# The low parts of all weights on GpSimd: a two-block hybrid layer stack on one core

## The reference, cut to what matters

```python
def first_block(x, ...):                      # block 1
    for l in range(2):
        h = _rmsnorm(x, norm_g[l])
        (u_a, v_a, z_a, c_q, c_kv, k_r, z_b, q_c, k_c, v_c, g_c, z_c, gate_logits) = _split_cols(h @ w_in[l])
        y_a = _spatial_gating(u_a, v_a, z_a, ...)
        y_b = _mla(c_q, c_kv, k_r, z_b, ...)          # 8 heads, attention causal by chunks
        y_c = _gla(q_c, k_c, v_c, g_c, z_c, ...)      # gated linear attention, 4 heads
        gates = jax.nn.sigmoid(gate_logits + b_gate[l]).reshape(bn, s, N_BRANCH, d)
        merged = (gates[:, :, 0] * (y_a @ w_branch[l, 0]) + gates[:, :, 1] * (y_b @ w_branch[l, 1])
                  + gates[:, :, 2] * (y_c @ w_branch[l, 2]))
        x = x + merged @ w_out[l]
def hybrid_layer(x, mem, ...):                # block 2, twice
    proj = rms_norm(x, norm_g) @ w_in         # a_q a_k a_v a_g b_q b_k b_v b_g m_q m_g
    # oa: attention over blocks of keys, ob: dilated attention, om: attention over 256 memory rows (mem @ w_mem_kv)
    y = concat([oa * silu(a_g), ob * silu(b_g), om * silu(m_g)])
    return x + y @ w_out
```

## Time and profile before

| | us |
|---|---|
| runs (3) | 1699.03, 1702.03, 1704.10; median 1702.03 |
| profiled execution | 1697.58, span of its instructions 1695.8 |
| TensorE busy | 1619.6 (96%) |
| VectorE busy | 1010.1 (60%) |
| ScalarE busy | 729.2 (43%) |
| GpSimd busy | 57.8 (3%) |
| granted TensorE clock | 0.995 of full |

### The profile page before, as it was taken

One profiled execution on the slowest core, in us unless ns is written; L12 is line 12 of the kernel. 1 busy time (PEld: TensorE's weight loads), 2 busy tenths in 40 slices (PEclk: granted clock), 3 DMA queues, 4 the chain that ended last, 5 costly groups with the idle time before them and its releaser, 6 DMA issues.

```text
span 1695.8 us, 21496 instructions
## 1 busy us (share of the span) xinstructions
PE 1619.6 (96%) x8009; PEld 1321.2 (78%) x8009; DVE 1010.1 (60%) x2246; ACT 729.2 (43%) x1503; POOL 57.8 (3%) x80
## 2 busy tenths in 40 slices
PE   6999999999999999999999999999989999997999
PEld 6878777787777878777787877898767779985667
DVE  4597656444444397757443344576886564778663
ACT  4444443333234443543332424434456553344662
POOL 0000002000001000002000001000000010000000
PEclk9999999999999999999999999999999999999999
DMA  7332121332323332112233323332112233211121
GB/s 219 96 87 75 39 61 53 97 98 90 98 89 89 92 92 87 51 50 63 75 96 91 100 87 112 94 84 68 61 33 68 81 87 99 81 49 45 38 75 62
DMA packets 80883, 136.23 MB, mean 80 GB/s; under 512 B 8190, under 2 KB 33420, under 8 KB 80780
## 3 DMA queue, kind: packets, MB, share of 16 engines
q1 hardware_dynamic: 77264, 129.48, 25.5%
q10 hardware_dynamic: 3516, 5.37, 1.1%
HBM read 132.74 MB, written 2.10 MB: 80 GB/s over the span
## 4 chain that ended last, share of the span: by engine, by line
PE 45%; DVE 13%; ACT 4%; issue 2%; POOL 0%; ACTq 0%; DVEq 0%
PE gemm_bank L695 34%; PE aux_bank L762 3%; PE aux_bank L791 3%; DVE w_lo L1340 2%; PE aux_bank L779 2%; DVE rope L1439 1%; ACT w_hi L1021 1%; DVE head_sums L1392 1%; DVE probs L1495 1%; ACT probs L1068 1%; DVE kT L1479 1%; PE aux_bank L750 1%; DVE probs L1507 1%; DVE product L1758 0%; ACT L1293 0%
## 5 line engine op out<-in xcount | busy, mean ns | idle before, releaser
L1021 ACT ACTIVATE w_hi<-raw 128x512 fp32r<-128x512 f32 (+3 forms) x524 | 305.5, 587 | 681.5 <-PE gemm_bank L695 680.1
L1340 DVE TENSOR_TENSOR w_lo<-raw,w_hi 128x512 fp32r<-128x512 f32 (+3 forms) x524 | 330.7, 636 | 445.0 <-ACT w_hi L1021 443.3
L695 PE MATMUL gemm_bank<-act_hi,w_hi 128*128 128x512 f32 x768 | 318.4, 415 | 14.9 <-DVE product L1758 3.8
L695 PE MATMUL gemm_bank<-act_hi,w_lo 128*128 128x512 f32 x768 | 300.8, 392 | 0.0
L695 PE MATMUL gemm_bank<-act_lo,w_hi 128*128 128x512 f32 x768 | 300.2, 391 | 0.0
L695 PE MATMUL gemm_bank<-w_hi,act_hi 128*128 128x384 f32 (+3 forms) x736 | 269.1, 366 | 6.5 <-DVE bq L1380 2.9
L695 PE MATMUL gemm_bank<-w_hi,act_lo 128*128 128x384 f32 (+3 forms) x736 | 257.4, 350 | 0.0
L695 PE MATMUL gemm_bank<-w_lo,act_hi 128*128 128x384 f32 (+3 forms) x736 | 257.4, 350 | 0.0
L695 PEld LDWEIGHTS gemm_bank<-act_hi,w_hi 128*128 128x128 f32 x768 | 144.6, 188 | 57.1 <-issue 12.7
L695 PEld LDWEIGHTS gemm_bank<-act_lo,w_hi 128*128 128x128 f32 x768 | 144.9, 189 | 31.1 <-issue 2.9
L695 PEld LDWEIGHTS gemm_bank<-act_hi,w_lo 128*128 128x128 f32 x768 | 144.5, 188 | 31.1
(11 more groups left out here) (289 smaller groups left out, 2133.7 us busy)
## 6 DMA issues: line engine op xcount, KB each, us to landing
raw<-in_w_in SPq DMA_DIRECT2D x104, 512.0 KB, 3.6
raw<-in_w_in SPq DMA_DIRECT2D x64, 384.0 KB, 3.3
raw<-in_w_out SPq DMA_DIRECT2D x32, 512.0 KB, 3.7
raw<-in_w_branch SPq DMA_DIRECT2D x24, 512.0 KB, 3.8
raw<-in_w_mem_kv SPq DMA_DIRECT2D x8, 512.0 KB, 3.7
raw<-in_w_in SPq DMA_DIRECT2D x16, 256.0 KB, 2.7
raw<-in_w_in SPq DMA_DIRECT2D x8, 416.0 KB, 4.9
x<-in_x SPq DMA_DIRECT2D x4, 512.0 KB, 5.2
```

The source lines that it names most:

```text
L695: last = pe.matmul(o, a, c, start=begin and n == 0, stop=end and n == 2)
L1021: act.activation(w_hi[:, s % RING, 0:n], raw[:, p % RAW, kk % PIECE, 0:n], ACT.Copy)\
L1340: dve.tensor_tensor(w_lo[:, s % RING, 0:n], raw[:, p % RAW, kk % PIECE, 0:n], w_hi[:, s % RING, 0:n].bitcast(F32), ALU.subtract).then_inc( ...
```

## The change

`residue` moves from VectorE's program to GpSimd's, with its `Splitter`; VectorE has none any more, and all its `split` calls go, so its order is that of its other work alone. `alongside` becomes plain draining of the generators. ScalarE, TensorE and SP are unchanged; `load_piece` still waits for `w_lo_ready`. On GpSimd the `split` calls stand between its own jobs.

```diff
@@ vector
-        def residue(s):
...
-        split = Splitter(residue)
@@ alongside
-            for gi in gis:
-                for kk in range(groups[gi].K):
-                    split.beside(gi, kk)
-                    for _ in range(per_step):
-                        next(work, None)
+        def some(work, n):
+            for _ in range(n):
+                next(work, None)
@@ attention
-                split_beside(split, a, n, evict_beside)
+                for gi in a.side[n][1]:
+                    evict_beside(gi)
@@ block_1
-            alongside(work, [gi_of(1, l, n) for n in ("u", "za")], 2, at_end, False)
+            some(work, 32)
+            wait_gemm_read(dve, gi_of(1, l, "u"))
+            wait_gemm_read(dve, gi_of(1, l, "za"))
...
@@ block_2
-            alongside(a_heads, [gi_of(2, l, n) for n in ("av", "bq")], 2, at_end)
+            for _ in a_heads:
+                pass
+            evict(gi_of(2, l, "bq"), lambda b: flat_2("bq")[:, b, :])
@@ gpsimd
         def factors_x(before):
             for t in range(NT):
+                if t == NT - 1:
+                    split.to(split.at + 1)
                 pool.wait_ge(squares_ready, before + NT + t + 1)
...
+        def residue(st):
+            gi, kk = step_group[st]
+            p = first_piece[gi] + kk // PIECE
+            n = groups[gi].n
+            pool.wait_ge(w_hi_ready, st + 1)
+            pool.tensor_tensor(w_lo[:, st % RING, 0:n], raw[:, p % RAW, kk % PIECE, 0:n],
+                               w_hi[:, st % RING, 0:n].bitcast(F32), ALU.subtract).then_inc(w_lo_ready, 1)
+        split = Splitter(residue)
...
             else:
+                split.to(first_step[gi_of(1, l - 1, "out", 1)] + KD)
                 factors_x(NT + 2 * NT * (l - 1))
+            split.beside(gi_of(1, l, "v"), 3)
             pool.wait_ge(sums_ready, 3 * l + 1)
             factors(sums[:, 8:8 + 2 * NT], 8, 2 * NT, 1.0)
+            split.beside(gi_of(1, l, "u"), 0)
             pool.wait_ge(sums_ready, 3 * l + 2)
             factors(mean_var[:, :, 1], 0, NT, 1.0)
+            split.beside(gi_of(1, l, "zc"), 2)
             pool.wait_ge(yb_lo_ready, MH // 2 * (l + 1))
             pool.memset(kt_pad[:, :, :, :], 0.0).then_inc(pads_zeroed, 1)
+            split.through(gi_of(1, l, "zc"))
             pool.wait_ge(gla_qk, 2 * l + 2)
...
+            split.beside(gi_of(1, l, ("gate", 0, 0)), 4)
             pool.wait_ge(sums_ready, 3 * l + 3)
             factors(sums[:, 0:NT * GH], 0, NT * GH, 1.0 / DV)
         for l in range(DEPTH):
+            split.through(gi_of(*out, "out", 0))
             pool.wait_ge(squares_ready, before + NMEM // P)
             factors(sums[:, 64:64 + NMEM // P], 64, NMEM // P, 1.0)
             if l == 0:
+                split.beside(gi_of(*out, "out", 1), 3)
                 aux_wait_full(pool, (2, 0, "mem", KD - 1))
                 pool.memset(kT_2[:, :, :, :], 0.0).then_inc(keys_zeroed, 1)
+            split.to(first_step[gi_of(*out, "out", 1)] + KD)
             factors_x(before + NMEM // P)
+        split.to(len(step_group))
```

More of the change, by code:

```diff
@@ L1356, in scale_x, with features @@
                .then_inc(rows_scaled, 1)
-        def features(key, ks, n_cols, hi, lo, gain=None, k0=0, after=lambda kk: None):
+        def features(key, ks, n_cols, hi, lo, gain=None, k0=0):
             for kk in ks:
@@ L1370, in features, with evict @@
                 ins.then_inc(read_of((*key, kk)), 1)
[L1371 to L1377, removed]
+        def evict(gi, dst, rows=P):
             for b in range(groups[gi].banks):
@@ L1563, in block_1 @@
             job = 3 * l - 1
-            g_c = first_step[gi_of(1, l, "c")]
             for t in range(NT):
                 scale_x(l, t)
-            split.to(g_c + 1)
-            features((1, l, "x"), range(KD), T, act_hi, act_lo, vec_col(R_X + KD * l, KD),
-                     after=lambda kk: split.to(g_c + 1 + (kk + 1) // 2) if kk < 6 else None)
+            features((1, l, "x"), range(KD), T, act_hi, act_lo, vec_col(R_X + KD * l, KD))
             if l == 0:
                 rope_angles()
-            split.through(gi_of(1, l, "c"))
             wait_gemm_read(dve, gi_of(1, l, "c"))
-            split.beside(gi_of(1, l, "v"), 2)
             for t in range(NT):
@@ L1585, in block_1 @@
                         ins.then_inc(sums_ready, 1)
-            split.beside(gi_of(1, l, "v"), 5)
             dve.wait_ge(rstd_ready, job + 2)
@@ L1663, in prepare @@
                 heads_done()
[L1665 to L1670, removed]
             a = attention_1(l)
             work = prepare()
-            alongside(work, [gi_of(1, l, n) for n in ("u", "za")], 2, at_end, False)
+            some(work, 32)
+            wait_gemm_read(dve, gi_of(1, l, "u"))
+            wait_gemm_read(dve, gi_of(1, l, "za"))
+            for g in range(4):
+                mark(dve.tensor_tensor(u[:, g, :], u[:, g, :], za[:, g, :], ALU.mult))
             def sum_out(g):
@@ L1689, in block_1 @@
                     begin(a, *event)
-                split.beside(gi_of(1, l, "zb"), kk)
-                for _ in range(3):
-                    next(work, None)
+                some(work, 3)
                 if kk == 6:
@@ L1699, in beside_mla @@
                 dst = {"qkc": qk_c, "vc": vc}[group_key[gi][2]]
[L1700 removed]
+                evict(gi, lambda b: dst[:, b, :])
             def gate_out(p, bank, read):
@@ L1728, in block_1 @@
                                   ALU.subtract).then_inc(yb_lo_ready, 1)
-            alongside(gates, [g_zc], 1)
+            for _ in gates:
+                pass
             gla(l)
-            g_00 = [gi_of(1, l, ("gate", 0, 0)), gi_of(1, l, "branch", 0, 0)]
-            alongside(gla_rows(l), g_00, 1)
+            for _ in gla_rows(l):
+                pass
             merge(l, 0, 0)
@@ L1782, in tail @@
                 scale_rows(mem_x[nxt], mem_n[nxt], NMEM // P, 3 * DEPTH + nxt + 1, 64, mem_scaled)
-            split.beside(out_1, 3)
             if nxt is not None:
                 features((2, nxt, "mem"), range(KD), NMEM, mem_hi[nxt], mem_lo[nxt], vec_col(R_MEM + KD * nxt, KD))
-            split.to(first_step[out_1] + KD)
             for t in range(NT):
-                if t == NT - 1:
-                    split.to(first_step[out_1] + KD + 1)
                 update_x(out_1, 1, t)
@@ L1794, in tail @@
             mkv = gi_of(2, nxt, "mkv")
-            split.beside(mkv, 0)
             for t in range(NT):
                 scale_x(DEPTH + nxt, t)
-                split.beside(mkv, min(t, 3))
             features(key, range(4), T, act_hi, act_lo, gain)
-            split.beside(mkv, 5)
             features(key, range(4, 6), T, act_hi, act_lo, gain)
-            split.through(mkv)
             features(key, range(6, KD), T, act_hi, act_lo, gain)
@@ L1973, in block_2 @@
                     begin(a, *event)
-                split.beside(gi_of(2, l, "bk"), kk)
             def drain(g):
@@ L2065, in _ @@
             before = NT + 2 * NT * (DEPTH - 1) + (2 * NT + NMEM // P) * l
+            out = (1, DEPTH - 1) if l == 0 else (2, l - 1)
+            split.through(gi_of(*out, "out", 0))
             pool.wait_ge(squares_ready, before + NMEM // P)
```

22 lines of the change are left out of this document (2 added, 20 removed).

## The result

| | before | after |
|---|---|---|
| median of the runs | 1700.53 us (4 runs) | 1732.12 us (4 runs) |
| profiled execution | 1697.58, span 1695.8 | 1731.23, span 1729.4 |
| granted TensorE clock | 0.995 | 0.988 |

The changed kernel is slower by 1.9%: ratio 1.0186, 95% interval 1.0163 to 1.0208. The forecast was 1716 with 1706 to 1728 of its own. The direction was right; the time lies 16 us above the forecast and 4 above the range.

What follows compares the result with a forecast made beforehand. TensorE, busy 96% of the span, was the bound; only its 76 us of standing could change. Terms summed to +16.7 us: 1714.3 from the profiled 1697.6, 1718.7 from the median 1702.0, middle 1716, range 1706 to 1728.

Steps and rivals of the forecast that it cites:

- rival 1: GpSimd yields and VectorE is never held, showing in block 2's attention and the bq copy: -24 us, 1678; chance 0.22.
- rival 2: SBUF reading is shared, not exclusive; a hit costs VectorE about 0.6 us: -6 us, 1696; chance 0.24.
- 4: Fourth rival: little moves, because VectorE's lateness has other causes; the middle of rival 2, no separate chance.
- Rival 3: GpSimd gets too few turns, TensorE waits 5 us for low parts in each of four long stretches: 1735; chance 0.04.
- (a): Rotations before bq in block 2: held VectorE work outweighs removed subtractions, +4.0 us a layer, +8.
- (b): VectorE's preparation of block 1's heads: heads ready 4.6 us later against slack 2.8, +1.3 us a layer, +2.6.
- GLA: Gated linear attention: its two memsets come one low part later, given back by VectorE's free queue; priced at 0.
- (c): Merges, eight with alternating product and addition: low parts block additions, last product 0.5 us later each, +4.
- (d): Turns into block 2 and its second layer: out and mkv low parts late, x_n scalings held, +7.7 us.
- (e): Attentions: subtractions and standing removed outweigh held work; block 2 -1.5 us a layer, -3; block 1 -1.
- (f): First merge: no longer behind o_tok's low parts, so its 1.6 us wait goes, -1.6.
- the middle between the two scales: Forecast time 1716, between 1714.3 on the profiled execution's scale and 1718.7 on the median's.

## Why the prediction was right and wrong

**The mechanism was right.** A low part on GpSimd holds a two-input instruction of VectorE for about its rest, products out of PSUM and reductions not at all. Rivals 1, 2 and 4 fall: the durations that decide rival 1 are longer here, and unchanged only where GpSimd does not read, at 1678.2; a full hit costs 1.09 us and not rival 2's 0.6; and with 1.9% more time it is not little that moves. That this is rival 1's 1678 is partly chance: there VectorE's one-input work is held and low parts come late. Rival 3 falls: low parts are waited for 11.3 us, mostly at the turns; in the four long stretches it is some 1 us in each preparation and none before bq, where the rival had 5 each. Of what I said would show it, two things did not come. The waits for the probabilities stayed at 14.2 us, where I expected near 13. And the mean of the low part is 1.35, where I expected 1.5 to 1.7, because 212 of the 340 began while VectorE ran nothing.

**(a) about right.** TensorE waits 5.2 us a layer for bq, forecast 5 to 6: 7.5 more in all. The lag grows 10.1, forecast 8; the lower clock at the end of the wait and behind it, which the forecast did not have, is in the difference.

**(b) is the step that failed**: +2.6 forecast, +17.4 measured. The low parts hold the preparation of block 1's heads as forecast, but the term for it, 13 x 1.2 = 15.6 us a layer, was too small, and the lower clock behind the wait was no term at all. I can name three parts of the delay. I took 51.5 us of VectorE's preparation and let 13 of its 17 low parts hold it, 15.6 added to 10.4 removed. In the trace the preparation lasts 61.5 us (84.7 to 146.3) instead of 51.6: the removed part was 10.4 as forecast, so the added one is 20.3. First, a preparation that lasts longer meets more low parts, 21 and not 17; I had put that into (a) and left it out here. Second, 18 of the 21 hold something, by about 1.0 us each, where I had 13 of 17: only three fall on the reductions, not four, and held are also the normalization of v with its one input (544 to 1226 ns on the mean) and the tiny root steps (225 to 927). Third, VectorE began 0.8 later and waited 0.7 for ScalarE's squares at the reductions, where I had it start 0.6 earlier. So the heads came 10.7 us later, not 4.6; less the slack of 2.8, and less some 1.6 by which TensorE itself came later, that is the wait of 6.3. The fourth part is not in the heads at all: after standing that long TensorE ran at the lower clock, and the lag grew by a further 2.7 us in the first layer and 1.8 in the second. Undoing the place (-14.3) shows the whole; filling the pause shows the clock's part in its trace (2.6 and 1.7), not in the time.

**GLA: priced 0, measured +5.3.** This term was put at nothing. The cumulative sums have two inputs of 512 columns, `qk_c x e_st` two of 1024. The last one, for which TensorE waits, takes
```profile
272.82 2.13 DVE L1804 TENSOR_TENSOR qk_c<-qk_c,e_st 128x1024 f32<-128x1024 f32 x1
```
and before
```profile
261.26 1.22 DVE L1853 TENSOR_TENSOR qk_c<-qk_c,e_st 128x1024 f32<-128x1024 f32 x1
```
while three low parts in a row take 6.40 us from 267.47, so each waits as well. I had looked only at GpSimd's memsets there, not at what its low parts do to VectorE.

**(c) was too high**: +4 forecast for the merges, +1.0 in TensorE's waits for products (5.2 to 6.2), and with the 1.6 of the first merge the lag falls by 1.8. 14 of 32 additions are held by 0.39 us each, not by 1.2: the addition starts when more than half of the low part is over (0.54 us are left). That it does so because both follow TensorE's steps is argued, not shown.

**(d) right**: forecast 7.7, lag 8.3, undone -7.0 (8.3 by the ratios). **(e)** and **(f)** right in sign: -7.1 against -4, and the first merge's wait is gone; some 1.5 us of the -7.1 fall at 1535, where the clock is lowered in the kernel before alone. Of the middle between the two scales: the new runs stand at 1732.1 on the median and 1731.2 in the profile, which explains nothing of the miss.

Left over is the clock. The sum 16.7 + 14.8 in (b) + 5.3 in the GLA - 4.2 in (c) and (f) and some 1 in all others gives the 33.7; up to 12 of it are time at the lower clock, spread over these places, and not a place of their own.

## What to carry to other kernels

Before work is moved onto GpSimd, list for each stretch which VectorE instructions read two SBUF tiles, or scale or normalize one: each GpSimd instruction that reads SBUF can cost such a stretch nearly its own length (1.09 us here, with 1.23 of the low part left). Where the stretch has no idle time, more of them fall into it than you count at first, because the stretch grows (21, not 17). Move only the work that falls beside PSUM reads, reductions and waiting (here the low parts of the attentions, -0.4%); where VectorE was full, in the preparation, before bq and in the GLA, it cost more than the subtractions that it took off. And where a new wait of TensorE is long (5.2 and 6.3 us here), count the lower clock behind it too (1.8 to 2.7 us at each wait for the heads).

## What the hardware showed that I had not expected

- The lock works for both orders and for whole instructions: a VectorE instruction of 0.95 us took 2.04 when a low part with 1.23 to go was ahead of it, and GpSimd instructions that only write still hold VectorE's one-input scaling (`x_n` 734 to 976 ns) though not its two-input products.
- Behind a wait of 6.3 us TensorE was granted half its clock for some 6 us, in both layers; with the wait filled with unused matmuls it was not. Elsewhere in the kernel lowered stretches come and go between kernels that are the same up to there (548 to 558).
- A 0.67 us reader on GpSimd in place of a 1.35 us one is worth 67 us (1732.1 to 1665.0), more than taking all reads away and keeping it busy for 1.6 us (1678.2); up to 8 us of the difference between these two can be the clock.
